# Recurrent heads of a two-block decoder layer: each head on its own half of the rows, with state products of 64x64x64

## The reference

```python
def step(state, inp):
    r_t, w_t, k_t, v_t, kk_t, b_t = inp
    sa = jnp.einsum('bhvk,bhk->bhv', state, -kk_t)
    state = (state * w_t[:, :, None, :] + sa[..., None] * b_t[:, :, None, :]
             + v_t[..., None] * k_t[:, :, None, :])
    return state, jnp.einsum('bhvk,bhk->bhv', state, r_t)
```

## Time and profile before

| | us |
|---|---|
| median of 3 runs | 3125.29 |
| lowest and highest | 3121.56, 3127.32 |
| the profiled execution | 3122.08 |
| its span in the trace | 3120.3 |

### The profile page before, as it was taken

The page is one execution under the profiler, slowest core; times in us unless marked ns, Lnnn a source line. Parts: engine busy times, 40 slices in busy tenths (PEclk is TensorE's granted clock), DMA queues, the critical chain, the costliest instruction groups (busy, mean ns, idle before and its releaser), DMA issues.

```text
span 3120.3 us, 52395 instructions
## 1 busy us (share of the span) xinstructions
PE 3000.6 (96%) x21592; PEld 2668.4 (86%) x21592; DVE 1922.0 (62%) x2603; ACT 1537.8 (49%) x2132; POOL 160.7 (5%) x248
## 2 busy tenths in 40 slices
PE   8999999889899999999999999999999999999998
PEld 7888888767688887777999999999989989898896
DVE  6555555774777877787759844445655545445454
ACT  6444444454566666665443337654344434334343
POOL 0000000200000000000066300000000000000000
PEclk9999999989899999999999989999999999999999
DMA  6223223223688887886444434445555555545454
GB/s 231 95 96 109 104 101 106 84 91 115 236 320 317 324 321 295 306 323 228 163 166 159 154 122 164 163 179 214 189 188 192 188 189 189 189 163 189 167 187 147
DMA packets 81812, 581.94 MB, mean 187 GB/s; under 512 B 9009, under 2 KB 9265, under 8 KB 12338
## 3 DMA queue, kind: packets, MB, share of 16 engines
q1 hardware_dynamic: 79056, 566.45, 50.0%
q10 hardware_dynamic: 2530, 12.19, 1.0%
HBM read 574.41 MB, written 4.19 MB: 185 GB/s over the span
## 4 chain that ended last, share of the span: by engine, by line
PE 85%; DVE 10%; ACT 3%; issue 2%; DMA 0%; ACTq 0%; SPq 0%; DVEq 0%
PE PG L794 10%; PE PG L796 10%; PE PG L797 10%; PE PG L821 6%; PE PG L822 6%; PE PG L820 6%; PE PG L852 4%; PE PG L1232 4%; PE PG L1233 4%; PE PG L1234 4%; PE PG L853 3%; PE PG L854 3%; DVE ring_r L696 3%; PE PX L940 2%; PE PX L1284 1%
## 5 line engine op out<-in xcount | busy, mean ns | idle before, releaser
L696 DVE TENSOR_TENSOR ring_r<-ring,work_r 128x1024 fp32r<-128x1024 f32 x492 | 584.1, 1230 | 315.9 <-ACT work_r L689 312.5
L689 ACT ACTIVATE work_r<-ring 128x1024 fp32r<-128x1024 f32 x492 | 493.1, 1051 | 538.4 <-PE PG L797 291.8
L689 ACT ACTIVATE C_r<-ring 128x1024 fp32r<-128x1024 f32 x268 | 269.1, 1052 | 456.6 <-PE PG L797 333.8
L797 PE MATMUL PG<-YT_r,ring_r 128*128 128x256 f32 x1664 | 470.5, 283 | 0.0
L696 DVE TENSOR_TENSOR ring_r<-ring,C_r 128x1024 fp32r<-128x1024 f32 x268 | 319.7, 1234 | 222.0 <-ACT C_r L689 218.6
L797 PE MATMUL PG<-work_r,ring_r 128*128 128x256 f32 x1344 | 377.1, 281 | 0.0
L797 PEld LDWEIGHTS PG<-YT_r,ring_r 128*128 128x128 f32 x1664 | 317.1, 191 | 0.0
L854 PE MATMUL PG<-HT_r,ring_r 128*128 128x256 f32 x960 | 271.3, 283 | 0.0
L797 PEld LDWEIGHTS PG<-work_r,ring_r 128*128 128x128 f32 x1344 | 254.7, 190 | 0.0
L821 PE MATMUL PG<-ring_r,HT_r 128*128 128x512 f32 x624 | 246.6, 395 | 0.0
L794 PE MATMUL PG<-YT_r,C_r 128*128 128x256 f32 x832 | 239.3, 288 | 6.3 <-DVE ring_r L696 6.3
(11 more groups left out here) (650 smaller groups left out, 7189.5 us busy)
## 6 DMA issues: line engine op xcount, KB each, us to landing
ring<-weights SPq DMA_DIRECT2D x472, 1024.0 KB, 4.8
C<-weights SPq DMA_DIRECT2D x32, 1024.0 KB, 4.9
work<-weights SPq DMA_DIRECT2D x32, 1024.0 KB, 5.2
work<-xT SPq DMA_DIRECT2D x4, 512.0 KB, 7.3
XT<-x ACTq DMA_DIRECT2D x1, 2048.0 KB, 7.9
residual<-XT ACTq DMA_DIRECT2D x4, 512.0 KB, 3.0
XT<-residual ACTq DMA_DIRECT2D x1, 2048.0 KB, 11.2
result<-YT SPq DMA_DIRECT2D x8, 256.0 KB, 4.1
```

The lines of the kernel that those rows point to most:

```text
L689: act.activation(w_high(u)[:, c], weights(u)[:, c], ACT.Copy).then_inc(w_hi, 1)
L696: dve.tensor_tensor(w_low(u)[:, c], weights(u)[:, c], w_high(u)[:, c].bitcast(F32), ALU.subtract).then_inc(w_lo, 1)
L797: last = pe.matmul(o, wl, high[:, k, :], start=False, stop=(n == kts - 1), skip_group_check=True)
```

## The change

Each head now has its own half of the rows everywhere: tokens, features, state and results.

- `TOK` becomes twelve 64x64 blocks for each half (`VTOK_`, `BTOK`, `KTOK`). The six transposes become 24 products of 64x64x64 with the constant `ident64`.
- The products of `sco` and `ksco` write the row half of their head, no longer that of their chunk; the banks are divided by pairs of chunks. Their number and shapes stay.
- The state `ZB` has 64 columns and no zero blocks. `W`, `U`, `Y` and `Z` consist of 64x64x64 products, the two heads in turn.
- `Z{c}` is issued and signalled ahead of `Y` (except in the last chunk), so its filling now stands between `Z` and `Y`, and `Y` is followed directly by the next `W`.
- ScalarE's copies to `W_` and `U_` are 128 rows by 64 columns. VectorE's update of the state is one instruction for c = 0 and two for the others, where it was one and three; the first of the two now waits for itself through `link`.

```diff
-                for n in range(6):
-                    src = (V_, BT_, KT_)[n // 2]
-                    mm = pe.transpose(PX[:, n // 4, (n % 4) * P:(n % 4) * P + P], src[:, (n % 2) * P:(n % 2) * P + P],
-                                      con("ident"))
+                for n in range(3 * NCH):
+                    src, c = (V_, BT_, KT_)[n // NCH], n % NCH
+                    for hs in HEADS:
+                        mm = pe.matmul(PX[hs, n // 8, n % 8 * CH:n % 8 * CH + CH], src[hs, c * CH:c * CH + CH],
+                                       con("ident64")[hs, :], start=True, stop=True)
...
-                        rows, cs = slice(64 * (c % 2), 64 * (c % 2) + 64), slice(64 * (c % 2), 64 * (c % 2) + 64)
-                        for h in range(2):
-                            hs = slice(64 * h, 64 * h + 64)
-                            o = PX[rows, 2 + h, P * (c // 2):P * (c // 2) + P].rearrange("p (a n) -> p a n", a=2)
+                        cs = slice(64 * (c % 2), 64 * (c % 2) + 64)
+                        for hs in HEADS:
+                            o = PX[hs, 2 + c // 2, P * (c % 2):P * (c % 2) + P].rearrange("p (a n) -> p a n", a=2)
                             mm = pe.matmul(o, keys[hs, c * CH:c * CH + CH], AR[hs, c // 2, :, cs], start=True, stop=True)
...
                         dve(p, f"z{c - 1}")
-                        pe.matmul(PX[rows, 0, 0:P], AR[:, tt, 0, cs], z, start=True, stop=False, skip_group_check=True)
-                    for h in range(2):
-                        mm = pe.matmul(PX[rows, 0, 64 * h:64 * h + 64], MKK[rows, h, tt, 0, :],
-                                       TOK[rows, tt, 64 * h:64 * h + 64], start=(c == 0), stop=(c == 0 or h == 1),
-                                       skip_group_check=True)
+                        for hs in HEADS:
+                            pe.matmul(PX[hs, 0, 0:CH], AR[hs, tt, 0, cs], z[hs, :], start=True, stop=False)
+                    for hs in HEADS:
+                        mm = pe.matmul(PX[hs, 0, 0:CH], MKK[hs, c, 0, :], VTOK_[hs, c, :], start=(c == 0), stop=True)
                     done(mm, p, f"W{c}")
                     act(p, f"W{c}")
-                    for h in range(2):
-                        mm = pe.matmul(PX[rows, 1, 64 * h:64 * h + 64], Q_[rows, 2 * h + tt, :],
-                                       W_[rows, 64 * h:64 * h + 64], start=True, stop=True)
+                    for hs in HEADS:
+                        mm = pe.matmul(PX[hs, 1, 0:CH], Q_[hs, c, :], W_[hs, :], start=True, stop=True)
                     done(mm, p, f"U{c}")
                     act(p, f"U{c}")
+                    if c + 1 < NCH:
+                        for hs in HEADS:
+                            pe.matmul(PX[hs, 2, 0:CH], BTOK[hs, c, :], U_[hs, :], start=True, stop=False)
+                        for hs in HEADS:
+                            mm = pe.matmul(PX[hs, 2, 0:CH], KTOK[hs, c, :], VTOK_[hs, c, :], start=False, stop=True)
+                        done(mm, p, f"Z{c}")
...
-                        pe.matmul(PX[:, 3, c * CH:c * CH + CH], z, AR[:, tt, 1, cs], start=True, stop=False,
-                                  skip_group_check=True)
...
+                        for hs in HEADS:
+                            pe.matmul(y[hs, :], z[hs, :], AR[hs, tt, 1, cs], start=True, stop=False, skip_group_check=True)
+                    for hs in HEADS:
+                        pe.matmul(y[hs, :], U_[hs, :], MBK[hs, c, 1, :], start=(c == 0), stop=False, skip_group_check=True)
+                    for hs in HEADS:
+                        mm = pe.matmul(y[hs, :], VTOK_[hs, c, :], MKK[hs, c, 1, :], start=False, stop=True,
                                        skip_group_check=True)
-                    if c + 1 < NCH:
-                        pe.matmul(PX[:, 2, 0:P], TOK[rows, 2 + tt, :], U_[rows, :], start=True, stop=False)
-                        mm = pe.matmul(PX[:, 2, 0:P], TOK[rows, 4 + tt, :], TOK[rows, tt, :], start=False, stop=True)
-                    done(mm, p, f"Z{c}")
+                    if c + 1 == NCH:
+                        done(mm, p, f"Z{c}")
...
-                        dve.tensor_scalar(ZP, ZB[:, c % 2, :], end, None, ALU.mult)
+                        link(dve.tensor_scalar(ZP, ZB[:, c % 2, :], end, None, ALU.mult))
                     pe(p, f"Z{c}")
-                    new, old = (ZT, ZB[:, (c + 1) % 2, :]) if c else (ZB[:, 1, :], None)
-                    ins = dve.scalar_tensor_tensor(new, PX[:, 2, 0:P], end, con("head64"), ALU.mult, ALU.mult)
+                    new = ZB[:, (c + 1) % 2, :]
                     if c:
-                        link(ins)
-                        ins = dve.tensor_tensor(old, ZT, ZP, ALU.add)
+                        ins = dve.scalar_tensor_tensor(new, PX[:, 2, 0:CH], end, ZP, ALU.mult, ALU.add)
+                    else:
+                        ins = dve.tensor_scalar(new, PX[:, 2, 0:CH], end, None, ALU.mult)
```

## The result

The changed kernel takes 3098.27 us (median of 4 runs, 3095.45 to 3101.64), the kernel before 3125.43 us beside it (4 runs, 3121.56 to 3127.32): a ratio of 0.9918, interval 0.9906 to 0.993. The profiled execution took 3101.64 us, the slowest of its four; that of before was 3.3 us faster than its median. So the two traces differ by 20.5 us only, and the rest of the 27.2 us is the choice of the executions (20.5 + 3.4 + 3.3).

A forecast was written before the change was run, and what follows sets the result against it. TensorE was taken as the bound, busy 3000.6 of 3120.3 us. Gains of 5.6 us (pairs 2 to 6), 0.7 (pair 1), 0 (pair 0) and 1.5 (pair 7) summed to 7.8: 3125.3 to 3117.5 us, range 3110 to 3124.

The forecast's parts named there:

- should only shift: All stages after the recurrence: they wait relative to what stands before them, so no gain or loss was counted there.
- `tok` less the wait before `sco`: Token transposes in pairs 2 to 6: 1.09 us longer, 0.68 us of it filling TensorE's wait, so 0.41 us remain.
- `U0`, `U3` with the waits behind them: State steps of the recurrence: 0.10 us less each, lost in the wait for a late ScalarE copy, so counted as zero.
- case (c): Recurrence: longer restarts behind waits and shorter ScalarE copies add up to 0.3 us a pair, 3115 us; inside the forecast.
- VectorE's shorter update of the state: Recurrence: worth nothing by itself, since VectorE stood idle 31.4 us for `Z`; put at zero.
- The wait before `sco`: TensorE waiting for VectorE's `bon`, 0.68 us a pair: filled by the longer `tok`, with `bon` starting no later.
- Rival (b): Wait before `sco` stays, 3.7 us, 3121 us; or single rounds save nothing and 128-column rounds take 0.25 us; 24%.
- the single rounds: Groups of one round, `W0` and each `U`: 0.475 us instead of 0.57, bounds 0.475 and 0.57.
- A round of 128 columns: Products in the new `sco` and `ksco`: four rounds at 0.225 us, 0.90 us; bounds 0.88 and 1.76.
- Pair 0's new wait: Before `U3`, for ScalarE's copy of `W3`, as TensorE arrives 0.8 us sooner: 0.6 us, so pair 0 comes out even.
- rival (d): New waits behind `U2` in all pairs, 0.6 us lost seven times; with a late `bon` 3122 to 3127 us; 6%.
- Rival (a): Rounds of two halves in one bank take turns: 6.2 us a pair, 50 us in all, 3167 us; 5%.

## Why the prediction was right and wrong

**The step that failed** is the sentence that later stages "should only shift". It took what TensorE's loop costs at its returns for the same in both kernels, without a reason. Of the 27.2 us, 10.7 are the recurrence; the remaining 16.5 are the two returns, by the medians of that comparison (the kernel before had medians from 3121.8 to 3125.4 in different comparisons, which leaves 13 to 16.5; the two traces give 14.7). The change added 1049 instructions to TensorE's queue ahead of the loop, and so moved the loop's head from slot 200 to 225, away from the one place that gave the long gap. The evidence that there was something to lose or win stood in the trace of before: its list of waits had 14.1 us of "issue" at L794, twice 7 us, and the granted clock fell to half behind it. I cut the list of waits to the stretch of the recurrence, and so didn't price it. That list doesn't tell that a shift of 25 slots would end it. But it was a term of up to 15 us beside a sum of 7.8, and it belonged in the range as a rival of its own.

**The sum for the recurrence held in its direction and most of its terms**, and was too small by 2.9 us (10.7 against 7.8). Per pair, in us, pairs 2 to 6:

| term | forecast | measured |
|---|---|---|
| `tok` less the wait before `sco` | +0.41 | +0.40 |
| `sco` | +0.68 | +0.59 |
| `ksco` | +0.46 | +0.43 |
| `W0`, `U1`, `U2` | -0.30 | -0.34 |
| `U0`, `U3` with the waits behind them | 0 | -0.23 |
| `W1` | -0.35 | -0.36 |
| `Y0`, `Z0` | -0.25 | -0.26 |
| `Y` with `W`, twice | -1.61 | -1.64 |
| `Y3` | -0.145 | -0.26 |
| sum | -1.11 | -1.67 |

The sum is the pairs' distance (-1.67), and five such pairs, 0.56 us each over the forecast, make 2.8 of the 2.9 us. Pair 7 gains 1.6 us in the two traces (the lead goes from 7.9 to 9.5 us), where 1.5 were forecast; pairs 0 and 1 can't be judged from them, because of the clock in pair 1 and since the changed kernel comes to pair 0 0.8 us later (62.93 against 62.14 us). At least 0.09 us off are three terms, 0.44 us together. The gain at `U0` and `U3` was not lost in the wait behind them: those waits went from 0.45 to 0.51 us and from 0.58 to 0.51, instead of growing by 0.1 each. ScalarE's copy is shorter, as case (c) had it, by 49 ns at the median. Its group before and after (min, median, max in ns):

```profile
L1645 ACT ACTIVATE work<-PX x32: 252/272/274, 90.0 to 541.3; 64x128 f32<-64x128 f32 x32
```
```profile
L1646 ACT ACTIVATE work<-PX x32: 205/223/225, 92.6 to 531.9; 128x64 f32<-128x64 f32 x32
```

At `U0` that is all of the gain: the copy starts 1.13 us behind it in both traces (in pair 1, 149.19 behind 148.06 before, 152.57 behind 151.44 after), and 0.05 us are saved. At `U3` the copy also starts sooner, 1.13 us behind it instead of 1.25 (172.94 behind 171.81, against 172.22 behind 170.97), which makes 0.18 us. `sco` measured 1.69 us, where I had 1.72, against 1.10 before when its restart behind the wait is counted, which I hadn't done; `Y3`'s saving was sized without its restart too. These are the longer restarts and shorter copies of (c), which I had placed inside of the forecast but given 0.3 us a pair; they came to 0.44, and the other terms to 0.12.

**Point by point.** VectorE's shorter update of the state was put at zero, and nothing speaks against it: nothing in the list of waits ends with it. The wait before `sco` was to vanish under a longer `tok`, with `bon` not moving: `bon` starts at 183.87 us, 0.4 us after 183.47, and `tok` itself starts 0.41 us later (179.99 against 179.58), so it moved with its pair and not with the 1.1 us that `tok` grew. It is done at 184.29, `sco` starts at 184.77, no idle time between. Rival (b) is out, by this and by the single rounds: they cost 0.46 us (forecast 0.475, bounds 0.475 to 0.57). A round of 128 columns cost (1.22 - 0.36) / 4 = 0.215 us (forecast 0.225), by `ksco`. Pair 0's new wait is 0.4 us, forecast 0.6; in no other pair did one appear, so rival (d) is out. Rival (a) is refuted: rounds of two halves into one bank start 0.115 us apart at L1002 to L984, and `tok`'s twelve took about 1.4 us and not 2.6. Here the measurement decides against the rule in the Trainium skill, TensorEngine Tiling (Array Packing), Gotcha 1: PSUM Pressure, for this form.

**What the rule on instruction fetch says.** The cost of a return is first what the rows show, 7.1 us or 1.6. The Trainium skill, Runtime: NRT & Kernel Launch, section Instruction fetch mechanics, says that instructions come in blocks of 256 (16 KiB), that prefetch is purely sequential, and that "Branching breaks sequential prefetch": a target outside of the window is fetched before work goes on. The profile's page of the kernel before agrees on the block's size: its queue of instructions moved 2.90 MB in 177 packets, 16.4 KB each. The rule gives every return a stall and doesn't say that it can be 1.6 or 7.1 us for one instruction's difference; the long one, by the packets above, takes one block more.

## What to carry to other kernels

Before pricing an edit of a long unrolled part, look for "issue" gaps in the whole list of waits, and for branches behind the edit. An edit that adds or removes instructions shifts every later loop head in that engine's program, and that can be worth more than the edit: here 13 to 16.5 us beside 10.7. Compare both versions once with the loop written out, or with the head at the same place, before giving the difference to the edit; where such a gap stands at the return of a loop of few rounds, try the loop written out.

## What the runs showed of the hardware

- The same branch back costs 1.6 to 2.1 us or 7.0 to 7.1 us. Slot 200 of the built program gave 7 us in two different kernels; 201, 224 and 225 gave 1.6 to 2.1. With the head placed by hand, 128 and 0 gave 1.7, and 200 and 239 split the cost in two gaps (1.8 + 2.0, 1.6 + 4.2). Each long gap goes with one more packet of the instruction queue (177 packets against 175, 182 against 180). That the built slot 200 is the last of its block fits all of these; no run shows directly where the program stands in memory.
- Idle for 7.1 us, TensorE came back at a granted clock of 0.50; idle for 1.6 us, at 1.00 in the changed kernel. Each long gap so costs about 2 us more than its length. A short one isn't always free of this: in the kernel before with 25 instructions more the clock was 0.50 for 3.4 us, from 2735.6 us, behind an idle 1.8 us.
- Two products of 64x64x64 in full float32 run at once on the diagonal quarters in one bank, 0.115 us a round; four on the four quarters, with 128 columns, took 0.44 us for eight.
- 231 instructions of nothing but satisfied waits at the start delayed the first product from 11.56 to 26.44 us.
